# Two-layer hybrid block on one core: the last output projection in runs of two weight pieces per token block, and the norm behind it block by block

## The chip, the cores and the metric

The kernel runs on one core of a Trainium2 chip. The metric is the device time of one execution in microseconds; the number given for a kernel is the median of its runs. The kernel before was timed in three runs: 1341.96, 1341.98 and 1348.33 us, median 1341.98 us. A core has TensorE (matmuls and transposes, into PSUM), VectorE, ScalarE and GpSimd (elementwise work) and SyncE, which here only issues DMAs.

## The reference

Input `x` is 256 tokens by 1024 features in float32. It goes through a state-space layer and an attention layer, each with a feed-forward, and then through a second block: a chunked state-space branch and a windowed-attention branch, gated and added, an output projection, and a gated feed-forward with a short convolution. Only the end matters here:

```python
merged = (jax.nn.sigmoid(g_ssd) * (y_ssd @ w_ssd_proj[l])
          + jax.nn.sigmoid(g_attn) * (y_attn @ w_attn_proj[l]))
x = x + merged @ w_out[l]                 # w_out: 1024 x 1024
h2 = rms_norm_2(x, norm2_g[l])
u = causal_dwconv(h2 @ w_up[l], ffn_conv_w[l], ffn_conv_b[l])   # w_up: 1024 x 5632
u_gate, u_val = jnp.split(u, 2, axis=-1)
x = x + (jax.nn.silu(u_gate) * u_val) @ w_down[l]               # w_down: 2816 x 1024
```

`rms_norm_2(x, g)` is `x * rsqrt(mean(x*x) + 1e-6) * g`, row by row.

## The kernel before, in words

**Split products.** Every float32 product is made of three matmuls: each operand is split into a high part (rounded to the fast format) and a low part (the rest), and high times high, high times low and low times high are added up in PSUM. `XH` and `XL` are the high and low part of the transposed activations, `HI` and `LO` those of the weights.

**Tokens.** The 256 tokens are two token blocks of 128 (`tb` 0 and 1). `h` is the running sum, `y` a scratch of the same shape, `acc` the PSUM accumulator of both blocks (four banks), `wk` four more banks.

**Weight pieces.** All weights come in numbered pieces of 128 x 2048 values (the down pieces of the last feed-forward are half that size). `P_WOUT2` is 143, so pieces 143 to 146 are the output projection `w_out_2` (in the prediction: its pieces 0 to 3), two blocks of 128 input features each, and 147 and 148 are the first two of the feed-forward's up weights (pieces 4 and 5). SyncE loads a piece in two halves, a and b, into one of two raw slots (`load`, L320 to L330, the DMA is L329), and before each half waits until the low part of the piece two earlier is done. ScalarE copies the halves to `HI` (`hi_next`, L1400 to L1408) when they have landed and the piece four earlier has been used by TensorE. The low parts, `LO = raw - HI` (L462), are made by VectorE for half a (`lo_next`, `lo_to`) and by GpSimd for half b (`upto`). TensorE waits for both (`arrived`, L589) and counts a piece as done with `used`.

**Order.** Each engine's program is written out by hand, in one fixed order, and the engines meet at semaphores. So what waits on an engine holds up all that is behind it in that engine's program.

**The stage before the change's.** TensorE ends the state-space branch's projection (`group_out`, twice, matmuls of L685). VectorE then multiplies `acc` by the gate and adds it to `y`, block 0 and then block 1 (L2641 to L2650).

**The output projection.** `norm_transpose(5)` (L691 to L702, L1340) turns `y` into four quarters: quarter q belongs to token block q // 2 and holds four blocks of 128 features, four transposes each (L701), into bank q of `wk`. ScalarE's `xT_high(5)` (copy, L1453) and VectorE's `xT_low(5)` (subtract, L1981) make `XH` and `XL` from each quarter. Then the loop at L1341 takes the four pieces: `down` (L671 to L689) does for each piece block 0 and then block 1, 12 matmuls each of 512 columns (L685), 96 in all. After block 0 of the last piece it raises `acc_first`, on which VectorE adds block 0 to `h` (L2661), and after the last matmul block 1.

**The norm and the feed-forward's input.** ScalarE sums the squares of `h` (`pre(4)`, L1888, instructions of L1424: both blocks); GpSimd makes the reciprocal root of each block (`row_rstd(9)`, L506 and L507, at L568, behind the low parts of half b up to piece 148); VectorE multiplies (`pre(5, 9)`, L1967); TensorE transposes four quarters (`norm_transpose(6, 6, 4)`, L1347); ScalarE copies all four (`xT_high(6)`, L1889), VectorE makes the four low parts (`xT_low(6)`, L2663). `ffn_up(0, 0)` then waits for the third and fourth of these (`xT_wait`) and starts the up matmuls (L601 to L603). The numbers 6 and 4 are fillers: matmuls of zeros (`keep_busy`, L661 to L664, 512 columns in bfloat16) ahead of the transposes of block 0 and ahead of those of block 1.

The same arrangement in blocks stands elsewhere in the kernel: in the attention layer's first projection `norm_transpose(2, 14, 0, (0, 1))` (L908) is followed by block 0's matmuls, then `norm_transpose(2, 0, 0, (2, 3))` (L944) and block 1's. The norms in front of the first two feed-forwards (`norm_transpose(1 + 2 * layer, 20, 2)`, L858) are made as norm 6 is.

Of the kernel before, what the change touches and what calls it, by code (L numbers as in the profile page):

```python
# [15 lines left out]
P = 128  # L16
SEQ = 256
TB = SEQ // P
D = 1024
KD = D // P  # L20
# [104 lines left out]
def build(nc, ins, out):  # L125
    ctx = ExitStack()
    with ctx:
# [5 lines left out]
        def S(name):  # L133
            if name not in sems:
                sems[name] = ctx.enter_context(nc.semaphore(name))
            return sems[name]
# [3 lines left out]
        HI = sb("HI", [P, 4, 2048], F32R)  # L140
        LO = sb("LO", [P, 4, 2048], F32R)
        X2 = sb("X2", [P, KD, 2, SEQ], F32R)
        XH, XL = X2[:, :, 0, :], X2[:, :, 1, :]
# [441 lines left out]
        def _(pe):  # L585
# [3 lines left out]
            def arrived():  # L589
                s, _, piece = ring.next()  # L590
                pe.wait_ge(S("lo_a"), piece + 1)
                pe.wait_ge(S("lo_b"), piece + 1)
                return s

            def used(ins):

                ins.then_inc(S("piece_done"), 1)
# [73 lines left out]
            def down(s, tiles, last_group, kt=2, first=False, norm=None):  # L671


                for tb in range(TB):
                    ts = slice(tb * P, (tb + 1) * P)
                    for kk in range(kt):
                        xh, xl = tiles(kk)
                        if norm is not None:
                            xT_wait(norm[0], tb, norm[1] + kk)
                        stop = last_group and kk == kt - 1  # L680
                        for lhs, w, begin, end in ((xh, HI, first and kk == 0, False), (xh, LO, False, False),
                                                   (xl, HI, False, stop)):
                            for n in range(2):
                                c = kk * 1024 + n * 512
                                last = mm(acc[:, tb, n * 512:(n + 1) * 512], lhs[:, ts], w[:, s, c:c + 512],  # L685
                                          start=begin, stop=end, skip_group_check=True)
                    if last_group and tb == 0:
                        last.then_inc(S("acc_first"), 1)
                return last  # L689

            def norm_transpose(n, meanwhile=0, between=0, quarters=range(4)):  # L691

                keep_busy(wk[:, 3, :], meanwhile)
                for q in quarters:
                    tb, b = q // 2, q % 2
                    if q == 2:
                        keep_busy(wk[:, 3, :], between)
                    pe.wait_ge(S("y_ready"), 4 * n + q + 1)
                    for kk in range(4):
                        k = 4 * b + kk  # L700
                        last = nc.tensor.transpose(wk[:, q, kk * P:(kk + 1) * P], y[:, tb, k * P:(k + 1) * P], ident)  # L701
                    last.then_inc(S("xT_psum"), 1)  # L702
# [634 lines left out]
            group_out(SG, 0)  # L1337
            group_out(SG + 1, 1, True)

            norm_transpose(5)  # L1340
            for p in range(4):  # L1341
                s = arrived()
                used(down(s, lambda kk: (XH[:, 2 * p + kk, :], XL[:, 2 * p + kk, :]), p == 3, first=p == 0,
                          norm=(5, 2 * p)))


            norm_transpose(6, 6, 4)  # L1347

            def ffn_up(c, bank):
                if not (isinstance(c, int) and c < 4):  # L1350
# [29 lines left out]
        def _(act):  # L1380
# [63 lines left out]
            def pre(j):  # L1444

                for tb in range(TB):
                    pre_block(j, tb)

            def xT_high(n, quarters=range(4)):
                for q in quarters:  # L1450
                    tb, b = q // 2, q % 2
                    act.wait_ge(S("xT_psum"), 4 * n + q + 1)
                    A(XH[:, 4 * b:4 * b + 4, tb * P:(tb + 1) * P], wk[:, q, :].rearrange("p (k t) -> p k t", k=4),  # L1453
                      ACT.Copy).then_inc(S("xT_hi"), 1)

                if 3 not in quarters:
                    return
                if 1 <= n < 5:
                    load_gpre(n + 1)
                if 1 <= n < 4:  # L1460
                    load_gpost(n)
# [423 lines left out]
            xT_high(5)  # L1885
            first = P_WOUT2 + 4
            hi_to(first + 1)
            pre(4)  # L1888
            xT_high(6)  # L1889
            hi_to(first + 2)  # L1890


# [36 lines left out]
        def _(dve):  # L1929
# [40 lines left out]
            def pre(n, e):  # L1970

                for tb in range(TB):
                    pre_block(n, e, tb)

            def xT_low(n, quarters=range(4)):

                for q in quarters:
                    tb, b = q // 2, q % 2
                    dve.wait_ge(S("xT_hi"), 4 * n + q + 1)
                    ks, ts = slice(4 * b, 4 * b + 4), slice(tb * P, (tb + 1) * P)  # L1980
                    TT(XL[:, ks, ts], wk[:, q, :].rearrange("p (k t) -> p k t", k=4), XH[:, ks, ts].bitcast(F32),  # L1981
                       ALU.subtract).then_inc(S("xT_lo"), 1)
# [672 lines left out]
            for tb in range(TB):  # L2655
# [3 lines left out]
                    done(first - 1)  # L2659
                for n in range(2):  # L2660
                    TT(halves(h, tb, n), halves(h, tb, n), halves(acc, tb, n), ALU.add).then_inc(S("h_ready"), 1)  # L2661
            pre(5, 9)
            xT_low(6)  # L2663
            lo_to(first + 2)


# [125 lines left out]
```

## Time and profile before

| | |
|---|---|
| median of three runs | 1341.98 us (1341.96 to 1348.33) |
| the profiled execution | 1347.69 us |
| its span, first to last instruction | 1345.8 us |
| TensorE / VectorE / ScalarE / GpSimd busy | 96% / 76% / 50% / 31% |
| TensorE's mean granted clock | 0.987 of full speed |

All rows are of the one profiled execution, with times counted from its first instruction. In a timeline each row is one or more like instructions in order: start, time from the first one's start to the last one's end (matmuls overlap in their pipeline, so this is longer than the distance to the next row), engine, line, operation, output and inputs, count, and in brackets how long the engine had been idle and what released it. In a row of windows there follow, behind the stretch, its length, the busy time and number of instructions of TensorE's matmuls, TensorE's weight loads, VectorE, ScalarE and GpSimd, then TensorE's granted clock (1.00 is 2.4 GHz, 0.50 is 1.2 GHz), the DMA engines' busy share and GB/s.

### The profile page before, as it was taken

The page shows a single profiled execution, that of the slowest core. Times are in us where ns is not written, and L with a number is a line of the kernel's source. Part 1 is how long each engine was busy: PE and PEld are TensorE (multiplying, and loading weights), DVE is VectorE, ACT ScalarE, POOL GpSimd, SP SyncE. Part 2 cuts the span into 40 slices and gives each one's busy share as a digit, 9 for nine tenths or more (in the row PEclk, how much of TensorE's full clock was granted, in tenths as well). Part 3 has the DMA queues.
Part 4 walks back from the last instruction along what each step waited for, and adds up shares of the span by engine and source line. Part 5 has one row for each costly group of instructions (what it writes and reads, how often), then busy time and mean ns, then how long its engine had stood idle before and what let it go on. Part 6 is the DMA issues. An engine that isn't in the chain of part 4 may idle for free.

```text
span 1345.8 us, 20924 instructions
## 1 busy us (share of the span) xinstructions
PE 1286.8 (96%) x7700; PEld 1096.1 (81%) x7700; DVE 1024.0 (76%) x1483; ACT 670.9 (50%) x1124; POOL 419.1 (31%) x215
## 2 busy tenths in 40 slices
PE   6998999998889999999999999999999989999998
PEld 5876888877667788887788888899999947899998
DVE  7986777776764777776687545499999985699997
ACT  5765444444454544444545444355554523455553
POOL 5014444433202544443435212210000002345553
PEclk9999999999889999999999899999999989999999
DMA  7045665645213455553657423354454324366663
GB/s 212 32 130 168 188 188 189 197 121 188 63 63 126 156 188 187 187 187 98 204 168 219 117 90 94 94 157 127 154 156 127 125 62 141 91 191 187 188 187 110
DMA packets 166364, 197.12 MB, mean 146 GB/s; under 512 B 9982, under 2 KB 131326, under 8 KB 166270
## 3 DMA queue, kind: packets, MB, share of 16 engines
q1 hardware_dynamic: 164939, 191.54, 46.1%
q10 hardware_dynamic: 1362, 4.74, 1.0%
q8 instruction: 40, 0.66, 0.2%
q14 instruction: 23, 0.18, 0.0%
HBM read 195.20 MB, written 1.05 MB: 146 GB/s over the span
## 4 chain that ended last, share of the span: by engine, by line
PE 68%; DVE 21%; ACT 4%; issue 3%; DMA 2%; POOL 1%; DVEq 0%; SPq 0%; ACTq 0%
PE acc L685 20%; PE wk L637 9%; PE wk L601 6%; PE wk L603 6%; PE wk L602 6%; PE wk L639 5%; DVE LO L1948 4%; DVE arena L2517 2%; PE wk L1163 1%; PE acc L601 1%; PE acc L898 1%; PE acc L1189 1%; PE acc L602 1%; PE acc L603 1%; DVE LO L462 1%
## 5 line engine op out<-in xcount | busy, mean ns | idle before, releaser
L462 POOL TENSOR_TENSOR LO<-raw,HI 128x1024 fp32r<-128x1024 f32 (+1 forms) x162 | 387.5, 2398 | 847.6 <-ACT HI L1408 770.1
L1408 ACT ACTIVATE HI<-raw 128x1024 fp32r<-128x1024 f32 (+3 forms) x382 | 365.2, 996 | 118.9 <-DMA raw<-in_w_in 34.5
L462 DVE TENSOR_TENSOR LO<-raw,HI 128x1024 fp32r<-128x1024 f32 (+1 forms) x160 | 263.3, 1648 | 97.8 <-ACT HI L1408 97.5
L601 PE MATMUL wk<-X,HI 128*128 128x256 f32 x784 | 224.7, 287 | 3.2 <-DVE X L1981 1.2
L602 PE MATMUL wk<-X,HI 128*128 128x256 f32 x784 | 222.0, 283 | 0.0
L603 PE MATMUL wk<-X,LO 128*128 128x256 f32 x784 | 222.0, 283 | 0.0
L637 PE MATMUL wk<-X,HI 128*128 128x512 f32 x512 | 183.7, 401 | 2.5 <-DVE X L1981 2.5
L601 PEld LDWEIGHTS wk<-X,HI 128*128 128x128 f32 x784 | 150.3, 192 | 6.8 <-issue 2.8
L602 PEld LDWEIGHTS wk<-X,HI 128*128 128x128 f32 x784 | 150.4, 192 | 0.8
L603 PEld LDWEIGHTS wk<-X,LO 128*128 128x128 f32 x784 | 150.4, 192 | 0.0
L639 PE MATMUL wk<-X,LO 128*128 128x256 f32 x512 | 144.3, 282 | 0.0
L685 PE MATMUL acc<-HI,HH 128*128 128x512 f32 x392 | 122.1, 393 | 3.8 <-DVE HL L2560 3.1
L685 PE MATMUL acc<-LO,HH 128*128 128x512 f32 x392 | 121.3, 390 | 0.0
L685 PE MATMUL acc<-HI,HL 128*128 128x512 f32 x392 | 121.0, 390 | 0.0
L637 PEld LDWEIGHTS wk<-X,HI 128*128 128x128 f32 x512 | 97.1, 190 | 26.4 <-issue 2.9
L639 PEld LDWEIGHTS wk<-X,LO 128*128 128x128 f32 x512 | 97.6, 191 | 1.1
L601 PE MATMUL wk<-HI,X 128*128 128x512 f32 x208 | 84.1, 404 | 4.2 <-DVE X L1981 4.2
L685 PEld LDWEIGHTS acc<-LO,HH 128*128 128x128 f32 x392 | 73.6, 188 | 15.9
L685 PEld LDWEIGHTS acc<-HI,HL 128*128 128x128 f32 x392 | 73.6, 188 | 15.8
L2239 DVE TENSOR_TENSOR HL<-arena,HH 128x512 fp32r<-128x512 f32 x32 | 84.0, 2626 | 2.8 <-ACT HH L1601 2.8
L685 PEld LDWEIGHTS acc<-HI,HH 128*128 128x128 f32 x392 | 69.5, 188 | 17.6 <-DVE HL L2560 4.0
L602 PE MATMUL wk<-LO,X 128*128 128x512 f32 x208 | 82.4, 396 | 0.0
(387 smaller groups left out, 2196.9 us busy)
## 6 DMA issues: line engine op xcount, KB each, us to landing
raw<-in_mlp_w SPq DMA_DIRECT2D x128, 512.0 KB, 3.8
raw<-in_w_in SPq DMA_DIRECT2D x100, 512.0 KB, 4.2
raw<-in_w_up SPq DMA_DIRECT2D x44, 512.0 KB, 3.9
raw<-in_w_down SPq DMA_DIRECT2D x44, 256.0 KB, 3.1
raw<-in_att_w_in SPq DMA_DIRECT2D x16, 512.0 KB, 3.9
raw<-in_w_ssd_proj SPq DMA_DIRECT2D x16, 512.0 KB, 3.7
raw<-in_att_w_out SPq DMA_DIRECT2D x8, 512.0 KB, 4.2
raw<-in_w_out SPq DMA_DIRECT2D x8, 512.0 KB, 4.2
```

Source lines behind the costliest of these rows:

```text
L462: tensor_tensor(LO[:, s, cs], raw[:, s % 2, "ab".index(part), 0:m], HI[:, s, cs].bitcast(F32), ALU.subtract).then_inc(S(f"lo_{part}"), 1)
L601: mm(o, lh, rh, start=start, stop=False, skip_group_check=skip)
L602: mm(o, lh, rl, start=False, stop=False, skip_group_check=skip)
L603: return mm(o, ll, rh, start=False, stop=stop, skip_group_check=skip)
L637: mm(o, HI[:, s, w:w + P], X2[:, k, :, :].rearrange("p r t -> p (r t)"), start=k == 0, stop=False, skip_group_check=True)
L639: last = mm(o[:, 0:SEQ], LO[:, s, w:w + P], XH[:, k, :], start=False, stop=k == KD - 1, skip_group_check=True)
L685: last = mm(acc[:, tb, n * 512:(n + 1) * 512], lhs[:, ts], w[:, s, c:c + 512], start=begin, stop=end, skip_group_check=True)
L898: last = mm(acc[:, tb, n * 512:(n + 1) * 512], lhs[:, par, kk, ts], w[:, slots[par], c:c + 512], start=False, stop=end, skip_group_check=True)
L1408: A(HI[:, s, j * m:(j + 1) * m], raw[:, s % 2, j, 0:m], ACT.Copy).then_inc(S(f"hi_{part}"), 1)
L1948: TT(LO[:, s, cs], raw[:, s % 2, "ab".index(part), :], HI[:, s, cs].bitcast(F32), ALU.subtract).then_inc(S(f"lo_{part}"), 1)
L2239: TT(HL[:, par, :, :], sq_b[:, par, :].rearrange("p (j t) -> p j t", j=2), HH[:, par, :, :].bitcast(F32), ALU.subtract).then_inc(S("hid_lo ...
L2517: STT(o, x, taps[j][k], o, ALU.mult, ALU.add)
```

## The change

TensorE's part is a new loop. It takes the projection's pieces in pairs, (0, 1) and then (2, 3), and in each pair does block 0 with both pieces, then block 1 with both: four runs of 24 matmuls. The transposes of quarters 0 and 1 of norm 5 come before the first run, those of quarters 2 and 3 before the second. `acc_first` is raised after the third run. Norm 6 is split in two calls: 4 fillers and the transposes of block 0, then 4 fillers and those of block 1. ScalarE takes the squares of block 0, the copies of quarters 0 and 1, the squares of block 1, the copies of quarters 2 and 3. VectorE adds block 0 to `h` and makes its norm product, adds block 1, makes the low parts of quarters 0 and 1, the norm product of block 1, and the low parts of quarters 2 and 3. SyncE's and GpSimd's programs stay as they are. The diff:

```diff
--- before.py
+++ after.py
@@ -1337,14 +1337,34 @@
             group_out(SG, 0)
             group_out(SG + 1, 1, True)
 
-            norm_transpose(5)
-            for p in range(4):
-                s = arrived()
-                used(down(s, lambda kk: (XH[:, 2 * p + kk, :], XL[:, 2 * p + kk, :]), p == 3, first=p == 0,
-                          norm=(5, 2 * p)))
-
-
-            norm_transpose(6, 6, 4)
+            def out_block(s, p, tb):
+
+                ts = slice(tb * P, (tb + 1) * P)
+                for q in (2 * p, 2 * p + 1):
+                    xT_wait(5, tb, q)
+                    for lhs, w, begin, end in ((XH, HI, q == 0, False), (XH, LO, False, False), (XL, HI, False, q == KD - 1)):
+                        for n in range(2):
+                            c = (q % 2) * 1024 + n * 512
+                            last = mm(acc[:, tb, n * 512:(n + 1) * 512], lhs[:, q, ts], w[:, s, c:c + 512],
+                                      start=begin, stop=end, skip_group_check=True)
+                return last
+
+            for p in (0, 2):
+                out_slots = []
+                for tb in range(TB):
+                    if p == 0:
+                        norm_transpose(5, 0, 0, (2 * tb, 2 * tb + 1))
+                    for n in range(2):
+                        if tb == 0:
+                            out_slots.append(arrived())
+                        last = out_block(out_slots[n], p + n, tb)
+                        if tb == 1:
+                            used(last)
+                    if p == 2 and tb == 0:
+                        last.then_inc(S("acc_first"), 1)
+
+            norm_transpose(6, 4, 0, (0, 1))
+            norm_transpose(6, 4, 0, (2, 3))
 
             def ffn_up(c, bank):
                 if not (isinstance(c, int) and c < 4):
@@ -1885,8 +1905,10 @@
             xT_high(5)
             first = P_WOUT2 + 4
             hi_to(first + 1)
-            pre(4)
-            xT_high(6)
+            pre_block(4, 0)
+            xT_high(6, (0, 1))
+            pre_block(4, 1)
+            xT_high(6, (2, 3))
             hi_to(first + 2)
 
 
@@ -2659,8 +2681,10 @@
                     done(first - 1)
                 for n in range(2):
                     TT(halves(h, tb, n), halves(h, tb, n), halves(acc, tb, n), ALU.add).then_inc(S("h_ready"), 1)
-            pre(5, 9)
-            xT_low(6)
+                if tb == 1:
+                    xT_low(6, (0, 1))
+                pre_block(5, 9, tb)
+            xT_low(6, (2, 3))
             lo_to(first + 2)
```

## Rows read from the trace of the kernel before

**Rows 1.** The page: busy by engine, chain by engine, GpSimd's low parts.

```profile
PE 1286.8 (96%) x7700; PEld 1096.1 (81%) x7700; DVE 1024.0 (76%) x1483; ACT 670.9 (50%) x1124; POOL 419.1 (31%) x215
...
PE 68%; DVE 21%; ACT 4%; issue 3%; DMA 2%; POOL 1%; DVEq 0%; SPq 0%; ACTq 0%
...
L462 POOL TENSOR_TENSOR LO<-raw,HI 128x1024 fp32r<-128x1024 f32 (+1 forms) x162 | 387.5, 2398 | 847.6 <-ACT HI L1408 770.1
```

**Rows 2.** Windows, the feed-forward: us, busy by engine, clock, DMA share, GB/s.

```profile
1160.00:1345.00 185.00, 181.95 (x1276) 170.52 (x1274) 163.06 (x199) 99.63 (x170) 86.69 (x41) 1.00 0.55 169
```

**Rows 3.** Timeline, TensorE: start, us, operation [idle before, releaser].

```profile
1123.61 1.26 PE L701 MATMUL wk<-cst,y 128*128 128x128 f32 x8 [1.23 <-DVE y L2650]
1124.90 0.70 PE L685 MATMUL acc<-HI,X 128*128 128x512 f32 x2
...
1146.77 1.47 PE L664 MATMUL wk<-zero_bf 128*128 128x512 bf16 x6
1148.97 1.32 PE L701 MATMUL wk<-cst,y 128*128 128x128 f32 x8 [0.73 <-DVE y L1967]
1150.12 1.03 PE L664 MATMUL wk<-zero_bf 128*128 128x512 bf16 x4
1151.31 1.32 PE L701 MATMUL wk<-cst,y 128*128 128x128 f32 x8 [0.16 <-DVE y L1967]
1153.86 0.36 PE L601 MATMUL wk<-X,HI 128*128 128x256 f32 x1 [1.23 <-DVE X L1981]
```

**Rows 4.** Timeline, VectorE, the same stretch.

```profile
1122.86 1.29 DVE L2650 TENSOR_TENSOR y<-y,arena 128x512 f32<-128x512 f32 x2
1124.07 2.48 DVE L1981 TENSOR_TENSOR X<-wk,X 128x512 fp32r<-128x512 f32 x4
1126.46 4.56 DVE L462 TENSOR_TENSOR LO<-raw,HI 128x1024 fp32r<-128x1024 f32 x2
1132.83 1.23 DVE L462 TENSOR_TENSOR LO<-raw,HI 128x1024 fp32r<-128x1024 f32 x1 [1.81 <-ACT HI L1408]
...
1150.49 1.42 DVE L1967 SCALAR_TENSOR_TENSOR y<-h,rstd,gpre 128x512 f32<-128x512 f32 x2 [0.92 <-POOL rstd L507]
1151.83 2.48 DVE L1981 TENSOR_TENSOR X<-wk,X 128x512 fp32r<-128x512 f32 x4
```

**Rows 5.** Timeline, ScalarE, the same stretch.

```profile
1121.98 1.09 ACT L1453 ACTIVATE X<-wk 128x512 fp32r<-128x512 f32 x2 [5.56 <-PE wk L701]
...
1131.74 1.06 ACT L1408 ACTIVATE HI<-raw 128x1024 fp32r<-128x1024 f32 x1 [4.34 <-DMA raw<-in_w_up]
1133.52 1.06 ACT L1408 ACTIVATE HI<-raw 128x1024 fp32r<-128x1024 f32 x1 [0.72 <-DMA raw<-in_w_up]
...
1147.69 0.63 ACT L1424 ACTIVATE arena<-h 128x512 f32<-128x512 f32 x1 [1.38 <-DVE h L2661]
...
1149.66 1.26 ACT L1453 ACTIVATE X<-wk 128x512 fp32r<-128x512 f32 x2 [0.64 <-PE wk L701]
```

**Rows 6.** Timeline, TensorE, the attention layer's first projection.

```profile
306.61 1.03 PE L701 MATMUL wk<-cst,y 128*128 128x128 f32 x8
308.62 0.50 PE L601 MATMUL wk<-HI,X 128*128 128x512 f32 x1 [0.98 <-DVE X L1981]
```

**Rows 7.** Timeline, SyncE's queue, the changed stretch.

```profile
1127.71 9.91 SPq L329 DMA_DIRECT2D raw<-in_w_up  x6
```

**Rows 8.** Timeline, TensorE, a longer gap in the attention layer.

```profile
347.57 1.75 PE L921 MATMUL acc<-cst,arena 128*128 128x128 f32 x7 [3.51 <-DVE arena L474]
```

**Rows 9.** Windows, columns as in rows 2: work behind gaps and norm chains.

```profile
114.80:118.20 3.40, 3.40 (x11) 2.92 (x12) 2.36 (x3) 3.40 (x4) 1.66 (x1) 0.51 0.98 311
327.00:329.60 2.60, 2.60 (x8) 2.12 (x9) 0.00 (x0) 0.71 (x2) 1.80 (x1) 0.50 0.89 299
347.60:353.60 6.00, 6.00 (x18) 5.04 (x19) 5.55 (x22) 1.85 (x3) 4.71 (x2) 0.50 0.51 139
...
448.00:452.00 4.00, 3.91 (x23) 3.49 (x24) 2.96 (x3) 3.73 (x4) 2.09 (x1) 1.00 0.92 287
```


## The prediction

> **What bounds the kernel now.** First the page: TensorE is busy 96% of the span and 68% of the chain of work that ended last; VectorE 21% [rows 1]. A share over 1345.8 us says nothing of one stretch, so next the windows. From 1160 to 1345 TensorE is busy 181.95 of 185 us at full clock, and most of the missing 3.05 us are the output's way out [rows 2]. So a delay of the feed-forward's first matmul moves the end one for one, and nothing later absorbs it. Two things are to be found: how much later or earlier that matmul (1153.86) starts, and at what clock.
>
> Then the timeline of TensorE over the changed stretch [rows 3]: late transposes of norm 5 at 1123.61, 96 projection matmuls from 1124.90 with no gap, fillers at 1146.77, two groups of transposes, first up matmul at 1153.86. The 96 take 21.87 us, 0.228 each: 2.73 us for one piece on one token block, 5.47 for a run of two pieces. The chain behind them takes 1153.86 - 1146.77 = 7.09 us.
>
> **Part 1, the start of the projection: no gain.** The first matmul waits for the low part of the first transposed quarter. ScalarE starts the copies at 1121.98 [rows 5], but VectorE is in the gating of block 1 until 1124.15 and makes the low parts only then (1124.07 by its overlapped start) [rows 4]. That order isn't changed, so 1124.90 stays; only TensorE's own transposes leave this place. 0 us, bounds -0.1 (0.62 us of low part from 1124.07, and a handover) to 0.
>
> **Part 2, block 1's transposes move in line: +2.0 us.** Today they fill time in which TensorE waits anyway. After the change they come behind 24 matmuls, at 1124.90 + 5.47 = 1130.4, and block 1's first matmul needs transpose, ScalarE's copy and VectorE's low part, one behind the other. The trace has this very form in an earlier projection, with 8 transposes between two token blocks: 306.61 to 308.62, 2.01 us, 0.98 of it idle [rows 6]. All 96 matmuls stay, so the projection ends at 1146.77 + 2.0 = 1148.8. Bounds: 1.03 (the transposes alone) to 2.1.
>
> **What waits behind these waits.** VectorE stands in the low parts of quarters 2 and 3 until about 1130.4 + 1.3 + 1.2 = 1132.9 (0.69 to the copy and 0.63 for it [rows 3, 5], then two of the four low parts that take 2.48 [rows 4]); behind it in its queue are the weights' low parts for pieces 2 and 3, which before began at 1126.46 [rows 4]. Piece 2's is ready at 1132.9 + 1.23 = 1134.1, and TensorE asks for it at 1148.8 - 10.9 = 1137.9: cover 3.8 us. Piece 3's: ScalarE converts it after its two late copies, to 1134.1. The two low parts before took 4.56 us together, against 2 x 1.23 alone, beside GpSimd's [rows 4]; with that surplus of 2.1 us on it, it is ready by 1137.7 at the latest, wanted at 1140.6. Both 0 us. SyncE's loads of the next weights wait for those low parts: the first goes out at 1134.1 instead of 1127.71 [rows 7]. By today's times from issue to conversion (4.0 us for the first half, 1.8 more for the next [rows 5]) the four halves of pieces 4 and 5 are there at about 1138.2, 1139.9, 1141.7 and 1143.5. TensorE wants them after 1153: hidden. But two other things stand behind them. VectorE's last low part ends at about 1144.6, and it then adds block 0 (accumulator ready at 1148.8 - 5.5 = 1143.3): 1.3 us late. GpSimd takes piece 5's second half (2.4 us in the mean [rows 1], 1144.6 to 1147.0) before it computes block 0's reciprocal root, so that comes at about 1148.1 and block 0's norm product is written 1148.1 to 1149.5. TensorE asks for it after its fillers, at 1149.7. Cover about 0.9 us for the first half: 0 us, at most +1.
>
> **Part 3, the chain behind the last matmul: +1.2 us.** ScalarE's queue decides. Today the squares of block 1 start at 1147.69 [rows 5], 0.92 us after the last matmul. After the change they stand behind the two copies of block 0's transposes. These transposes stand behind the last matmul and 4 fillers, so: fillers 0.9 us (0.225 each; the later 4 run 1.03 with the tail), transpose to copy 0.69 (1148.97 to 1149.66 [rows 3, 5]), two copies 1.1 (1.26 with the tail). Squares of block 1 at end + 2.7: 1.8 us later than now. From there squares, root and handovers to the norm product take 1150.49 - 1147.69 = 2.80, product to transposes 1151.31 - 1150.49 = 0.82, and transposes to first matmul 2.01 as in part 2. Sum 2.7 + 2.8 + 0.82 + 2.01 = 8.33 us, against 7.09 now. What is saved is in the last term: today VectorE makes four low parts in a row from 1151.83 and TensorE waits for the third; after, the first two are done early (2.01 in place of 1153.86 - 1151.31 = 2.55). Hardly more is to be had, since block 0's part was never the last to come. Bounds: +0.3 (fillers hidden) to +2.2 (cover of block 0 gone). Six fillers become four in front; today's are hidden, since TensorE idles a further 0.73 us for the norm product before 1148.97 [rows 3], and the four after aren't.
>
> **Part 4, the clock: +2.1 us.** After the second fillers (end near 1151.5) TensorE has nothing to do until block 1's transposes at about 1155.1: 3.5 us idle, then a further 1.1 beside 1.0 of transposes. Today's idle pieces are 0.73, 0.16 and 1.23, and the clock holds. The row nearest to the new gap is one of 3.51 us before 347.57 [rows 8]: the clock there fell to 1.2 GHz and stayed so for 6.0 us of the work behind it; another fall lasts 2.6 us from 327.0 [rows 9]. The row nearest in kind, the same norm chain at the first feed-forward, has 3.4 us at 0.51 behind it, and the third chain of this form has none [rows 9]. I take 3.4: work at half rate loses 1.7, and the transposes in the chain some 0.4 (four, at twice their 0.12 us). Bounds 0 to 6.0 / 2 + 0.4 = 3.4.
>
> The Trainium skill, TensorE: Matmul & The Clock Gate, section "HAM oscillation — how this bites in real kernels", says that waits between bursts of matmuls put TensorE back to the half rate, so that the next burst starts cold. By that rule part 4 is paid and the sum is 5.3; by the two chains of this form that stayed at full clock it is 3.2. The trace agrees with the rule at the 3.51 us gap, and shows no chain with so long a gap that kept its clock.
>
> **Sum.** 0 + 2.0 + 1.2 + 2.1 = +5.3 us. The rows are of an execution of 1347.69 us (span 1345.8), 5.71 above the median of the runs, 1341.98, and near the slowest of the three, 1348.33. I add the difference to both: profile 1353.0, median 1347.3, +0.39%. A measurement of this kernel can tell about 0.5%, 6.7 us, so the forecast is "same", on the slow side.
>
> **Rivals.**
> 1. The clock holds: parts 2 and 3 alone, +3.2, 1345.2 us. For it: the chains before 448 and 1153.86. Against it: the idle stretch is three times any of theirs. Chance 0.22.
> 2. The half clock outlasts the gap by long: slower. Place: the first up matmuls of the feed-forward, behind 1157. Each us at half clock there costs 0.5; with 3.2 + 0.4 paid, the bound of 6.7 is passed from 6.2 us on. The 6.0 us behind 347.6 come to 6.6, a second stretch of 3.4 makes 3.6 + 3.4 = 7.0: 1349.0 us. Against it: behind 327.0 and 114.8 dense matmuls had the full clock back in 2.6 and 3.4 us. Chance 0.18.
> 3. Late supply: the cover of 0.9 us at GpSimd's root, or of 2.9 to 3.8 us at the weights' low parts, is gone. For it: VectorE and GpSimd slow each other in just these instructions. With 1.5 us more than the forecast: 6.8, 1348.8. Chance 0.06.
> 4. The change works as its form suggests: block 1's transposes cost nothing and block 0's run under matmuls, so only the shortened end counts, -0.5: 1341.5. Against it: the program order puts block 0's transposes behind the last matmul, and ScalarE's copies before block 1's squares. Chance 0.05.
>
> **How the numbers follow.** Forecast 0.47, rivals 0.22, 0.18, 0.06, 0.05, and 0.02 for a gain from something not seen here. Same: 0.47 + 0.22 + 0.05 = 0.74. Slower: 0.24. Faster: 0.02. The range takes in rival 1 less the bounds of parts 2 and 3 (3.2 - 1.9 = +1.3) and rival 2 with the 1.5 us of rival 3 on top (7.0 + 1.5 = +8.5): 1343.3 to 1350.5.
>
> **What would show it.** Right, if in the changed profile the projection starts 1.0 to 1.4 us behind the last y of block 1, one group of 8 transposes with some 1 us of idle stands in its middle, its end is 2.0 later, ScalarE's squares of block 1 follow the copies of quarters 0 and 1, TensorE is idle some 3.5 us before the last transposes, the first up matmul comes 8.0 to 8.8 us behind the last projection matmul, and the granted clock just behind is near 0.5. Wrong, if block 1's squares start within 1 us of the last matmul, if matmuls wait for a low part of pieces 2 or 3, or if anything before 1124 or after the first turn of the feed-forward changed its length.

## The result, and the profile after

The changed kernel takes 1351.74 us in the median of 21 runs (1347.85 to 1357.60); the kernel before, run beside it, takes 1345.61 us in the median of 21 (1340.93 to 1352.42). The ratio is 1.0046, with a 95% interval of 1.0035 to 1.0058: 6.2 us slower (4.7 to 7.8). The forecast was +5.3 us on a level of 1341.98. The distance was about right and the level was not: the 21 runs of the kernel before, the three shown among them, have a median 3.6 us above that of the three. One run of a variant below, fillers at the first place, took 1597.62 us at a mean granted clock of 0.749 and is left out of that variant's ratio.

The profiled execution of the changed kernel took 1352.65 us, with a span of 1350.8. Its projection starts 1.81 us earlier than in the execution before, in stages that are the same in both, so times are compared from the first projection matmul on. From there to the last instruction it is 1350.8 - 1123.09 = 227.7 us, and before it was 1345.8 - 1124.90 = 220.9: 6.8 us more. TensorE's timeline of the changed kernel, over the stretch of [rows 3]:

```profile
1119.53 1.03 PE L701 MATMUL wk<-cst,y 128*128 128x128 f32 x8
1123.09 0.98 PE L1348 MATMUL acc<-HI,X 128*128 128x512 f32 x2 [2.52 <-DVE X L2003]
...
1130.24 1.04 PE L701 MATMUL wk<-cst,y 128*128 128x128 f32 x8
1132.26 0.74 PE L1348 MATMUL acc<-HI,X 128*128 128x512 f32 x2 [0.97 <-DVE X L2003]
...
1148.75 1.04 PE L664 MATMUL wk<-zero_bf 128*128 128x512 bf16 x4
1149.62 1.04 PE L701 MATMUL wk<-cst,y 128*128 128x128 f32 x8
1154.52 1.97 PE L701 MATMUL wk<-cst,y 128*128 128x128 f32 x8 [2.99 <-DVE y L1989]
1157.14 0.55 PE L601 MATMUL wk<-X,HI 128*128 128x256 f32 x1 [0.65 <-DVE X L2003]
...
1164.60 1.04 PE L668 MATMUL acc<-zero_bf 128*128 128x512 bf16 x4
```

And two rows that the comparison needs from the kernel before, its first transposes of norm 5 and the end of its first up piece (`clear_acc`):

```profile
1121.35 1.03 PE L701 MATMUL wk<-cst,y 128*128 128x128 f32 x8
...
1159.69 1.04 PE L668 MATMUL acc<-zero_bf 128*128 128x512 bf16 x4
```

From the first projection matmul to that point it was 1159.69 - 1124.90 = 34.8 us, and it is 1164.60 - 1123.09 = 41.5 us. The 6.7 us more split into five. They are all but 0.1 of the 6.8 us, so nothing behind this stretch absorbs or adds anything:

| part | before | after | more |
|---|---|---|---|
| first 24 matmuls | 5.5 | 1130.24 - 1123.09 = 7.15 | 1.7 |
| block 1's transposes in line | 0 | 1132.26 - 1130.24 = 2.02 | 2.0 |
| other 72 matmuls | 16.4 | 1148.75 - 1132.26 = 16.5 | 0.1 |
| last projection matmul to first up matmul | 7.1 | 1157.14 - 1148.75 = 8.4 | 1.3 |
| first up piece | 1159.69 - 1153.86 = 5.8 | 1164.60 - 1157.14 = 7.5 | 1.6 |

The first and the last part are the clock, and so is some half microsecond of the fourth, the last transposes. The windows of the changed kernel, with the columns of [rows 2]:

```profile
1119.60:1123.00 3.40, 0.96 (x9) 0.72 (x7) 3.26 (x7) 1.09 (x2) 0.00 (x0) 1.00 0.00 0
1123.10:1126.50 3.40, 3.40 (x9) 2.62 (x10) 0.44 (x1) 0.00 (x0) 0.00 (x0) 0.53 0.00 0
...
1154.50:1157.10 2.60, 1.97 (x8) 1.57 (x8) 1.32 (x2) 1.17 (x3) 0.00 (x0) 0.50 0.00 0
1157.20:1160.50 3.30, 3.30 (x16) 3.30 (x17) 1.87 (x2) 1.81 (x2) 1.41 (x1) 0.50 0.00 0
```

TensorE has little to do from 1119.6 to 1123.0 (0.96 us of transposes), and runs the first matmuls at 1.2 GHz (0.53). It has nothing to do for 2.99 us ahead of 1154.52, and has 1.2 GHz for the transposes behind that and for the 3.3 us of matmuls from 1157.2. The other engines show who waited. VectorE of the changed kernel, against [rows 4]:

```profile
1131.51 1.29 DVE L2003 TENSOR_TENSOR X<-wk,X 128x512 fp32r<-128x512 f32 x2 [7.97 <-ACT X L1473]
1132.71 2.35 DVE L462 TENSOR_TENSOR LO<-raw,HI 128x1024 fp32r<-128x1024 f32 x2
...
1147.88 1.42 DVE L1989 SCALAR_TENSOR_TENSOR y<-h,rstd,gpre 128x512 f32<-128x512 f32 x2 [2.45 <-POOL rstd L507]
1149.21 1.28 DVE L2683 TENSOR_TENSOR h<-h,acc 128x512 f32<-128x512 f32 x2
...
1153.71 1.42 DVE L1989 SCALAR_TENSOR_TENSOR y<-h,rstd,gpre 128x512 f32<-128x512 f32 x2 [1.53 <-POOL rstd L507]
```

ScalarE, against [rows 5]:

```profile
1150.26 1.08 ACT L1473 ACTIVATE X<-wk 128x512 fp32r<-128x512 f32 x2 [4.05 <-PE wk L701]
1151.23 0.63 ACT L1444 ACTIVATE arena<-h 128x512 f32<-128x512 f32 x1
```

GpSimd's low parts of the weights in the changed kernel:

```profile
1133.94 3.38 POOL L462 TENSOR_TENSOR LO<-raw,HI 128x1024 fp32r<-128x1024 f32 x1 [16.86 <-ACT HI L1428]
...
1144.34 2.40 POOL L462 TENSOR_TENSOR LO<-raw,HI 128x1024 fp32r<-128x1024 f32 x1 [1.18 <-ACT HI L1428]
```

The issues on SyncE's queue, against [rows 7]:

```profile
1133.96 9.76 SPq L329 DMA_DIRECT2D raw<-in_w_up  x6
```

VectorE stood 7.97 us for quarter 2, and made the weights' low parts at 1132.71, not right after the first matmuls. SyncE's first up weight goes out 10.9 us after the first projection matmul; before it was 2.8. ScalarE squares block 1 at 1151.23, right behind the copies of 1150.26: 2.48 us after the last matmul, where it was 0.92.

### The profile page after: what moved, and what is told of

The parts are those of the page before. It is cut to its first block, busy times and chain, and to the rows that moved or that the text cites. A ratio compares the mean times of both kernels' runs of the same rounds, so it can differ in the third digit from the quotient of the medians.

```text
span 1350.8 us, 20920 instructions
## 1 busy us (share of the span) xinstructions
PE 1289.6 (95%) x7698; PEld 1098.1 (81%) x7698; DVE 1019.8 (76%) x1483; ACT 670.8 (50%) x1124; POOL 422.7 (31%) x215
## 4 chain that ended last, share of the span: by engine, by line
PE 67%; DVE 22%; ACT 4%; issue 3%; DMA 2%; POOL 1%; DVEq 0%; SPq 0%; ACTq 0%
PE acc L685 18%; PE wk L637 9%; PE wk L601 6%; PE wk L602 6%; PE wk L603 6%; PE wk L639 4%; DVE LO L1970 4%; DVE arena L2539 2%; PE acc L1348 2%; PE wk L1163 1%; PE acc L601 1%; DVE LO L462 1%; PE acc L898 1%; PE acc L1189 1%; PE acc L602 1%
## 5 line engine op out<-in xcount | busy, mean ns | idle before, releaser
L462 DVE TENSOR_TENSOR LO<-raw,HI 128x1024 fp32r<-128x1024 f32 (+1 forms) x160 | 257.6, 1613 | 98.0 <-ACT HI L1428 97.7
```

The costliest lines, as they stand in the source:

```text
L462: tensor_tensor(LO[:, s, cs], raw[:, s % 2, "ab".index(part), 0:m], HI[:, s, cs].bitcast(F32), ALU.subtract).then_inc(S(f"lo_{part}"), 1)
```

## The experiments

The table gives, for one profiled execution of each, the time from the first projection matmul to the first up matmul (free of the few matmul records that are missing in some traces) and to the last instruction, the granted clock at the two places, and the ratio to the kernel before, timed on the same chip. The variants had 12 runs each, ScalarE's order undone 7. The intervals of the ratios are 3 to 6 us wide, so single terms are read from the traces.

| kernel | to first up, us | to the end, us | first run | behind the norm chain | ratio (95%) |
|---|---|---|---|---|---|
| before | 28.96 | 220.9 | full | full | 1 |
| changed | 34.05 | 227.7 | half | half | 1.0046 (1.0035 to 1.0058) |
| changed, again | 32.41 | 226.2 | full | half | 1.0046 (1.0029 to 1.0063) |
| runs only | 31.10 | 223.1 | full | full | 1.0031 (1.0013 to 1.0049) |
| chain only | 31.09 | 224.6 | full | half | 1.0039 (1.0023 to 1.0055) |
| changed, fillers at both places | 32.69 | 224.6 | full | full | 1.0029 (1.0017 to 1.0041) |
| changed, fillers at the first | 32.04 | 226.2 | full | half | 1.0042 (1.0025 to 1.0060) |
| changed, ScalarE's order undone | 33.26 | 227.3 | half | half | 1.0039 (1.0018 to 1.0061) |
| changed, ScalarE's and VectorE's undone | 31.13 | 223.1 | full | full | 1.0025 (1.0008 to 1.0041) |
| runs, transposes mid-run | 29.88 | 221.9 | full | full | 1.0015 (0.9996 to 1.0033) |
| runs, all transposes ahead | 28.97 | 221.0 | full | full | 1.0002 (0.9989 to 1.0015) |
| early block 0 | 28.25 | 220.3 | full | full | 0.9992 (0.9979 to 1.0005) |

**Runs only.** The projection of the changed kernel with the last norm of the kernel before:

```diff
-            norm_transpose(6, 4, 0, (0, 1))
-            norm_transpose(6, 4, 0, (2, 3))
+            norm_transpose(6, 6, 4)
...
-            pre_block(4, 0)
-            xT_high(6, (0, 1))
-            pre_block(4, 1)
-            xT_high(6, (2, 3))
+            pre(4)
+            xT_high(6)
...
-                if tb == 1:
-                    xT_low(6, (0, 1))
-                pre_block(5, 9, tb)
-            xT_low(6, (2, 3))
+            pre(5, 9)
+            xT_low(6)
```

> The projection in runs with block 1's transposes in line, the norm behind it as in the kernel before. Measured from the first projection matmul to the end of the first up piece (34.8 us in the kernel before, 41.5 in the changed one). Theory A (four separate terms: transposes in line 2.0, chain 1.3, and two clock falls of 1.7 and 1.6, each caused by an idle stretch of TensorE that the change opens): 34.8 + 2.0 + 1.7 = 38.5 us with a clock fall in the first run of matmuls, 36.8 if the clock holds; kernel +3.7 or +2.0 us. Rival B (the falls are chance and would also come without the idle stretches; only the order of the engines' queues costs): 36.8 us, no fall in the projection in particular. Rival C (all of the cost is in the norm chain): 34.8 us.

Measured: 31.10 us against 28.96, +2.1, and 1.0031. In this execution the clock held in the first run, though TensorE had idled as long as in the changed kernel.

TensorE's timeline of the runs alone:

```profile
1121.51 0.70 PE L1348 MATMUL acc<-HI,X 128*128 128x512 f32 x2 [2.52 <-DVE X L2000]
...
1127.06 1.04 PE L701 MATMUL wk<-cst,y 128*128 128x128 f32 x8
1129.07 0.73 PE L1348 MATMUL acc<-HI,X 128*128 128x512 f32 x2 [0.98 <-DVE X L2000]
```

The first run is 5.55 us here; the next matmul comes 2.01 us behind the start of the transposes. Rival C, all in the norm chain, is out.

**Chain only.** The same three hunks the other way round, in the kernel before.

> The norm behind the projection block by block, the projection piece by piece as in the kernel before. Theory A: projection 21.9 us, chain 8.4 to 8.9 (block 0 has only 2.7 us of matmuls as cover here in place of 5.5), first up piece 7.5 at half clock: 37.7 to 38.3 us in all, kernel +2.9 to +3.5 us. Rival B: 36.1 us, no clock fall. Rival D (the block form of the chain pays only with the longer cover and harms without it): chain 10 us or more.

TensorE's timeline of the chain alone, from block 0's transposes of norm 6 on:

```profile
1145.88 1.32 PE L701 MATMUL wk<-cst,y 128*128 128x128 f32 x8 [0.45 <-DVE y L1970]
...
1151.01 1.97 PE L701 MATMUL wk<-cst,y 128*128 128x128 f32 x8 [2.94 <-DVE y L1970]
1153.62 0.55 PE L601 MATMUL wk<-X,HI 128*128 128x256 f32 x1 [0.65 <-DVE X L1984]
```

ScalarE's first squares of block 1 in the same execution:

```profile
1147.73 0.62 ACT L1425 ACTIVATE arena<-h 128x512 f32<-128x512 f32 x1
```

Measured: 31.09 us, +2.1; with the matmuls at 21.9 (96 x 0.228) that is a chain of 9.2, outside the 8.4 to 8.9 expected. Block 0 has half the cover: its transposes wait for its norm product and start at 1145.88, 1.5 us behind the last matmul (1122.53 + 21.87 = 1144.4), against 0.87 in the changed kernel. The squares of block 1 still stand behind the copies (1147.73, 3.3 us behind the last matmul), and the gap of 2.94 us behind it brings the half clock. So the longer cover of the runs does help the chain, by 0.8 us, and the chain in this form loses all the same. Rival D asked for a chain of 10 us or more and isn't met.

**Fillers at both places.**

```diff
                         norm_transpose(5, 0, 0, (2 * tb, 2 * tb + 1))
+                        keep_busy(wk[:, 3, :], 10 if tb == 0 else 0)
...
-            norm_transpose(6, 4, 0, (2, 3))
+            norm_transpose(6, 17, 0, (2, 3))
```

> The changed kernel with 10 fillers between the transposes of quarters 0 and 1 of norm 5 and the first run, and 17 in place of 4 ahead of the last transposes of norm 6, which fills the two idle stretches. Theory A: no clock fall in either place, first run 5.5 us, chain 7.8, first up piece 5.8, in all 37.6 us in place of 41.5; kernel 3 to 4 us faster than the changed one and +2.5 to +3.2 us against the kernel before. Rival B: falls come or not as before, no steady gain over the changed kernel (+6).

TensorE's timeline with fillers at both places, from block 0's transposes of norm 6 on:

```profile
1148.36 1.32 PE L701 MATMUL wk<-cst,y 128*128 128x128 f32 x8 [0.34 <-DVE y L1990]
...
1153.49 1.32 PE L701 MATMUL wk<-cst,y 128*128 128x128 f32 x8
1155.65 0.36 PE L601 MATMUL wk<-X,HI 128*128 128x256 f32 x1 [0.84 <-DVE X L2004]
```

ScalarE's copy of the last half piece of weights in it, and below it VectorE's norm product of block 1:

```profile
1142.88 1.06 ACT L1429 ACTIVATE HI<-raw 128x1024 fp32r<-128x1024 f32 x1 [1.71 <-DMA raw<-in_w_up]
```

```profile
1152.68 1.41 DVE L1990 SCALAR_TENSOR_TENSOR y<-h,rstd,gpre 128x512 f32<-128x512 f32 x2 [1.32 <-POOL rstd L507]
```

Measured: full clock at both places. Of the 32.69 us to the first up matmul 24.0 are the projection (5.55 + 2.01 + 16.5), so the chain is 8.6, over the 7.8 expected. The fillers are not the reason: the last transposes start 0.81 us behind their norm product (1152.68 to 1153.49), as in the changed kernel (1153.71 to 1154.52). In this execution the second half of piece 5 landed late: ScalarE waited 1.71 us for it, where it had waited 0.67 in the changed kernel, and copied it 4.1 us ahead of the last matmul's end instead of 5.5. GpSimd's low part, block 0's root and its norm product came that much later, block 0's transposes waited 0.34 us for it, and all behind them is late by some 0.7 us. That is rival 3's late supply, in one execution and against a cover that was as thin as forecast. The kernel is at 1.0029, and the changed one at 1.0046. The intervals overlap from 1.0035 to 1.0041, so the gain of some 2.3 us is likely, not certain. From the first projection matmul to the end the traces show 224.6 us, against 227.7 and 226.2 in the two executions of the changed kernel.

**Fillers at the first place only.**

```diff
                         norm_transpose(5, 0, 0, (2 * tb, 2 * tb + 1))
+                        keep_busy(wk[:, 3, :], 10 if tb == 0 else 0)
```

> The changed kernel with the 10 fillers ahead of the first run only. Theory A: no clock fall in the projection (5.5 us for the first run), the fall behind the norm chain stays: 41.5 - 1.7 = 39.8 us over the stretch, kernel +4.5 to +5 us. Rival B (falls are chance): the first run falls or not as in the changed kernel, kernel +6.

TensorE's timeline with fillers at the first place: the first run and the transposes behind it, then the first up piece from its start to `clear_acc`:

```profile
1120.87 0.70 PE L1348 MATMUL acc<-HI,X 128*128 128x512 f32 x2 [0.37 <-DVE X L2004]
...
1126.43 1.04 PE L701 MATMUL wk<-cst,y 128*128 128x128 f32 x8
...
1152.91 0.55 PE L601 MATMUL wk<-X,HI 128*128 128x256 f32 x1 [0.46 <-DVE X L2004]
...
1160.96 1.04 PE L668 MATMUL acc<-zero_bf 128*128 128x512 bf16 x4
```

The first run takes 5.56 us, and the fall behind the chain stays: the first up piece takes 1160.96 - 1152.91 = 8.05 us in place of 5.8. The ratio, 1.0042, is too wide to tell the 1.7 us from nothing.

**The changed kernel again.** No edit.

> The changed kernel once more, on this chip, for the two clock falls and for its distance to the kernel before. Theory A: the fall behind the norm chain comes again (3.0 us idle); the one in the first run, behind 2.5 us idle, comes in some executions and not in others, so the stretch is 41.5 or 39.8 us, kernel +5.5 to +6.5 us in the median. Rival B: both falls can be missing, stretch 38 us.

TensorE's timeline of this second execution, the same points and the last transposes:

```profile
1122.67 0.70 PE L1348 MATMUL acc<-HI,X 128*128 128x512 f32 x2 [2.52 <-DVE X L2003]
...
1128.22 1.04 PE L701 MATMUL wk<-cst,y 128*128 128x128 f32 x8
...
1152.46 1.97 PE L701 MATMUL wk<-cst,y 128*128 128x128 f32 x8 [2.99 <-DVE y L1989]
...
1162.71 1.04 PE L668 MATMUL acc<-zero_bf 128*128 128x512 bf16 x4
```

The first run has the full clock here (5.55 us), behind the same idle of 2.52; the gap of 2.99 us ends in half clock again. The stretch is 1162.71 - 1122.67 = 40.0 us, +5.2. Over all executions profiled: behind 2.52 us idle ahead of the first run the clock fell in 2 of 6 (changed, ScalarE's order undone) and not in 4 (runs only, both orders undone, transposes mid-run, changed again); with fillers there, or with all transposes ahead, in 0 of 6. Two of six against none of six is too little to show that the idle stretch is the cause at this place. Behind the 2.4 to 3.0 us ahead of the last transposes it fell in 5 of 5 (changed twice, chain only, fillers at the first, ScalarE's order undone); with that idle filled or under 1.3 us, in none of the other seven, the kernel before among them. Rival B, falls by chance, is out for the second place and open for the first. Short idle is no safeguard in general: at the norm chain of the first feed-forward, which no variant changes, the clock fell in 3 of the 12 executions (the kernel before, changed again, ScalarE's order undone), and the longest idle there was 1.65 us in the kernel before.

**ScalarE's order undone.**

```diff
-            pre_block(4, 0)
-            xT_high(6, (0, 1))
-            pre_block(4, 1)
-            xT_high(6, (2, 3))
+            pre(4)
+            xT_high(6)
```

> The changed kernel, but ScalarE takes the squares of both blocks before the copies of quarters 0 and 1. Theory A: squares of block 1 start 1.3 us earlier, but VectorE's low parts of quarters 0 and 1 then end 0.7 us later and its norm product of block 1 stands behind them: the chain is 0.4 us shorter, 8.0 in place of 8.4, kernel +5.5 to +6 us. Rival E (ScalarE's order alone holds the chain): chain 7.1 us, 1.3 less than in the changed kernel.

ScalarE's timeline with its order undone, the first squares of block 1:

```profile
1147.89 0.63 ACT L1444 ACTIVATE arena<-h 128x512 f32<-128x512 f32 x1 [3.71 <-DVE h L2681]
```

VectorE's timeline of it, the add of block 1 and its norm product:

```profile
1147.18 1.28 DVE L2681 TENSOR_TENSOR h<-h,acc 128x512 f32<-128x512 f32 x2
...
1150.95 1.41 DVE L1987 SCALAR_TENSOR_TENSOR y<-h,rstd,gpre 128x512 f32<-128x512 f32 x2
```

GpSimd's timeline of it, the root of block 1:

```profile
1149.71 0.56 POOL L507 TENSOR_TENSOR rstd<-nv,half 128x1 f32<-128x1 f32 x1
```

Measured: 33.26 us to the first up matmul, 0.8 less than the changed kernel with both at half clock in the first run; 0.4 was expected. The squares of block 1 start at 1147.89, some 1.3 us behind the last matmul (its 33.26 us are 7.2 + 2.0 + 16.5 of projection and so 7.6 of chain, in place of 8.4), now held by VectorE's add of block 1 at 1147.18, which stands behind the late norm product of block 0. The norm product follows at 1150.95, 0.7 us behind the root (1149.71 + 0.56), since VectorE's low parts of quarters 0 and 1 stand ahead of it, as expected. It starts 4.3 us behind the last matmul in place of 5.0; the rest of the 0.8 is that the last transposes and what follows take 2.4 us in place of 2.6. Rival E, that ScalarE's order alone makes the whole 1.3 us, is out.

**ScalarE's and VectorE's order undone.** The same, and

```diff
-                if tb == 1:
-                    xT_low(6, (0, 1))
-                pre_block(5, 9, tb)
-            xT_low(6, (2, 3))
+            pre(5, 9)
+            xT_low(6)
```

> The changed kernel with ScalarE's and VectorE's order of the last norm as in the kernel before; only TensorE's part stays changed. Theory A: VectorE's add of block 1 still stands behind its late norm product of block 0 (root held up by GpSimd's weight part), so the chain is 7.4 to 7.6 us as in the run with ScalarE's order alone undone, 0.8 to 1.0 less than the changed kernel's 8.4. Rival G (VectorE's low parts ahead of the norm product cost as much as ScalarE's copies do): 7.1 us or less. Kernel +4.5 to +5.5 us.

TensorE's timeline with both orders undone, behind the last projection matmul:

```profile
1143.70 1.04 PE L664 MATMUL wk<-zero_bf 128*128 128x512 bf16 x4
...
1150.78 0.36 PE L601 MATMUL wk<-X,HI 128*128 128x256 f32 x1 [1.23 <-DVE X L2001]
```

Measured: a chain of 1150.78 - 1143.70 = 7.08 us, that of the kernel before. The expectation of 7.4 to 7.6 was wrong: it overlooked that this VectorE order adds both blocks before either norm product, so nothing stands before block 1's add. Rival G's time is met. Its reason, the low parts ahead of the norm product, is one of two in VectorE's order: with ScalarE's alone undone they put the norm product 0.7 us behind the root, and the late add of block 1 put the squares 0.4 us later than before (1.3 against 0.92). The split of TensorE's part costs nothing: all 1.3 us of the chain come from the order of ScalarE and VectorE, the half clock in its transposes included. With that order the idle of 3 us goes too: the longest left is 1.23, and the clock stays full.

**Transposes in the middle of the first run**, on the runs alone.

```diff
-                    if p == 0:
-                        norm_transpose(5, 0, 0, (2 * tb, 2 * tb + 1))
+                    if p == 0 and tb == 0:
+                        norm_transpose(5, 0, 0, (0, 1))
...
+                        if p == 0 and tb == 0 and n == 1:
+                            norm_transpose(5, 0, 0, (2, 3))
                         last = out_block(out_slots[n], p + n, tb)
```

> The runs alone (norm 6 as in the kernel before), but block 1's transposes stand in the middle of the first run, between its two pieces, so that ScalarE's copy and VectorE's low part of quarter 2 run under the 12 matmuls of its second piece. Theory A (of the 2.0 us of the transposes in line, 1.0 is TensorE's own work and 1.0 is the wait for the copy and the low part): no idle stretch between the blocks, over the stretch 34.8 + 1.0 = 35.8 us where the clock holds in the first run, 1.7 more where it falls; 1.0 less than the runs alone. Rival J (the copy and low part are late in any place, or the low parts of the weights then stand in their way): 36.8 us as in the runs alone.

TensorE's timeline with the transposes in the middle of the first run:

```profile
1125.97 1.04 PE L701 MATMUL wk<-cst,y 128*128 128x128 f32 x8
1126.76 0.70 PE L1348 MATMUL acc<-HI,X 128*128 128x512 f32 x2
```

Measured: 29.88 us, +0.9, and no idle between the blocks; the kernel's ratio, 1.0015 (0.9996 to 1.0033), can't tell it from nothing. The 2.0 us in line are 0.9 of TensorE's own and some 1.1 of waiting for the copy and the low part.

**All transposes ahead of the first run**, on the runs alone.

```diff
+            norm_transpose(5)
             for p in (0, 2):
...
-                    if p == 0:
-                        norm_transpose(5, 0, 0, (2 * tb, 2 * tb + 1))
```

> The projection in four runs of two pieces, but with all four quarters transposed ahead of the first run, and the norm behind it as in the kernel before. Theory A (the order of the runs itself is free; what costs is that block 1's transposes leave the place where TensorE waits anyway and open an idle stretch): from the first projection matmul to the end of the first up piece 34.8 us as in the kernel before, no clock fall in the first run, kernel within 0.3%. Rival F (the pairs themselves cost, by the later release of pieces and later weights): 36 us or more, seen as a wait for low parts of pieces 2 or 3.

TensorE's timeline of it, the first projection matmul and the first up matmul:

```profile
1123.24 0.70 PE L1348 MATMUL acc<-HI,X 128*128 128x512 f32 x2
...
1152.21 0.35 PE L601 MATMUL wk<-X,HI 128*128 128x256 f32 x1 [1.23 <-DVE X L1999]
```

Measured: 28.97 us, the kernel before to a hundredth, and 1.0002. The order of the runs costs nothing by itself, nor does the later release of the pieces; rival F is out.

**Early block 0.** On the last one, TensorE without fillers ahead of block 0's transposes, and quarter 0's low part ahead of block 1's norm product:

```diff
-            norm_transpose(6, 6, 4)
+            norm_transpose(6, 0, 0, (0, 1))
+            norm_transpose(6, 14, 0, (2, 3))
...
-            pre(5, 9)
-            xT_low(6)
+                if tb == 1:
+                    xT_low(6, (0,))
+                pre_block(5, 9, tb)
+            xT_low(6, (1, 2, 3))
```

> Pairs with all transposes of norm 5 ahead; behind the last matmul block 0's transposes without fillers in front, 14 fillers ahead of block 1's; ScalarE as in the kernel before; VectorE makes the low part of quarter 0 ahead of block 1's norm product and the others behind it. Theory A: the weights come early again, block 0's norm product is ready at the last matmul, the chain is 6.6 to 6.8 us in place of 7.1, no clock fall: 34.3 to 34.5 us over the stretch, kernel -0.3 to -0.5 us against the kernel before, too little to be told by its time. Rival H (block 0's root or the fillers come late): chain 7.1 us or more.

TensorE's timeline with block 0 early, behind the last projection matmul:

```profile
1146.33 1.03 PE L701 MATMUL wk<-cst,y 128*128 128x128 f32 x8
...
1152.70 0.35 PE L601 MATMUL wk<-X,HI 128*128 128x256 f32 x1 [0.84 <-DVE X L2000]
```

VectorE's timeline of it, block 0's norm product and the low part of quarter 0:

```profile
1144.29 1.42 DVE L1986 SCALAR_TENSOR_TENSOR y<-h,rstd,gpre 128x512 f32<-128x512 f32 x2 [1.92 <-POOL rstd L507]
...
1149.10 0.69 DVE L2000 TENSOR_TENSOR X<-wk,X 128x512 fp32r<-128x512 f32 x1 [1.28 <-ACT X L1472]
```

Measured: the chain is 1152.70 - 1146.33 = 6.4 us in place of 7.1, 0.2 to 0.4 better than expected. Block 0's norm product is done at 1145.71, before the last matmul, because the weights' parts are not late here; its transposes need no filler; the low part of quarter 0 fits into VectorE's wait for the root. 0.7 us is 0.05% of the kernel, and its time can't tell it: 0.9992 (0.9979 to 1.0005).

## Why the prediction was right and wrong

**The level, where it failed.** The step is the last one of the sum, "I add the difference to both: profile 1353.0, median 1347.3". The profile's 1353.0 met 1352.65, but by luck: from the first projection matmul on the changed execution was 6.8 us longer, not 5.3, and its projection started 1.8 us earlier, which the change has no part in. The median didn't meet: the three runs shown (1341.96, 1341.98, 1348.33) and the profile's 1347.69 spread over 6 us, and two equal low ones were taken for the level. Over 21 runs of the kernel before it is 1345.61, and its runs reach from 1340.93 to 1352.42. The range had no term for that. Of the 4.4 us between 1347.3 and 1351.74, 3.6 are this level and 0.8 the difference: with 5.3 us on 1345.61 the forecast is 1350.9. The spread lies ahead of the changed stretch: the first projection matmul comes between 1119.65 and 1124.90 us in the twelve profiles, behind stages that are the same in all, and the kernel before had the latest of them. It goes with the clock: of the 23 runs of the kernel before that stand beside the changed one's second twelve, the fastest (1340.39) had a mean granted clock of 0.995 and the slowest (1351.02) 0.985. That falls of the clock in those stages make the spread is read from this, and no run tests it.

**Part 1, 0 us: right for the start, wrong in what it left out.** The projection starts 1123.09 - 1119.53 = 3.56 us behind the first transposes of norm 5, and before it was 1124.90 - 1121.35 = 3.55. But the wait there was read for the time of the transposes alone: when they leave, the idle is 2.52 us in one piece, and in 2 of 6 executions the first run goes at 1.2 GHz, 1.7 us more. The sum put the clock at this place at nothing, without a reason. That the idle piece causes the fall here is likely by the other place, but not shown.

**Part 2, +2.0: right.** 2.02, 2.01 and 2.02 us in the traces, and +2.1 for the runs alone. Everything argued to be covered was: weights' low parts at 1132.71 took 2.35 us together, without GpSimd's surplus, and were ready by 1135.1, with pieces 2 and 3 wanted from 1137.9 on; GpSimd's part (1144.34 to 1146.74) held block 0's root, and the norm product came at 1147.88, 0.2 us before the estimate. Such times can be held against each other only because the projection started 1.8 us earlier and its first run took 1.7 us longer, so that it ended at 1148.75 where 1148.8 was forecast. In the second execution, without the fall, the projection is 2.1 us longer than before.

**Part 3, +1.2: 1.3 in the table, of which some 0.5 belongs to part 4.** Its terms were 2.7, 2.8, 0.82 and 2.01; measured 2.48, 2.48, 0.81 and 2.62. The first two are shorter than forecast, and the last one holds the transposes at half clock, which the forecast had in part 4. At full clock, with fillers at both places, that term took 2.16, so part 3 by its own terms is 2.48 + 2.48 + 0.81 + 2.16 - 7.09 = 0.8, and two errors nearly cancel. The mechanism, ScalarE's squares behind its copies, is shown by undoing it: -0.8 for ScalarE alone, -1.3 with VectorE.

**Part 4, +2.1: right, 1.6 behind the chain (up to 2.2 in the variants) plus 0.5 in it.** The fall came in all five executions with such a gap, 2.99 us in the changed kernel where 3.5 was forecast. By the Trainium skill's rule (TensorE: Matmul & The Clock Gate, "HAM oscillation — how this bites in real kernels") idle between bursts is followed by a cold start; the trace agrees, and shows that 2.4 to 3.0 us sufficed in five of five executions at this place, and 2.5 us in two of six ahead of the projection.

Of the rivals, the first (clock holds, +3.2) fell. The second (half clock for over 6.2 us behind 1157) asked for too much at one place: the first up piece lost 1.6 to 2.2 us, twice which is 3.3 to 4.4 us of half clock. The profiled execution still came to +6.7, with the second fall in the first run that no rival had. Late supply didn't come in the changed kernel's two profiles and did, by 0.7 us, in that of the fillers at both places. The free gain didn't come.

## What to carry to other kernels

Before moving work out of a place where an engine waits anyway, price the idle stretch that it leaves, at TensorE's clock as well as in time, and fill it where the clock matters. In a chain by halves, list each engine's order and look for a step of the last half that stands behind one of the first: here ScalarE's copies and VectorE's product of block 0 stood before block 1's squares and add, and block 0 was never the late one. And take the level of a forecast from many runs: three didn't fix it here. The change itself is best read from the first instruction that it touches to the last of the kernel, which leaves the spread of the stages ahead out.

## What was not expected of the hardware

TensorE idle for the same 2.52 us ahead of the same matmuls is followed by 1.2 GHz in two executions and by 2.4 GHz in four, and the first run takes 7.2 us in place of 5.55. The two low parts of VectorE took 4.56 us in the kernel before [rows 4] and 2.35 in the changed one, and it was GpSimd's, at 1133.94, that took 3.38 us this time where its mean is 2.4 [rows 1]. All twelve traces agree: 4.55 to 4.56 us for VectorE's two and 2.46 to 2.47 for GpSimd's in the four with all of norm 5's transposes ahead of the projection, 2.35 and 3.38 to 3.39 in the other eight. One of the two pays when they meet, and which one goes with when they start: in the kernel before GpSimd's starts at 1127.47, ahead of VectorE's second, and in the changed one at 1133.94, just behind it. No run tests this by itself.
